# Delta scan with one key product per pair of heads, and separate semaphores for bonus and gate

## The reference

```python
def wkv7_scan(S0, r, w, k, v, a, b):
    def step(S, inp):
        r_t, w_t, k_t, v_t, a_t, b_t = inp
        sa = jnp.einsum('bhij,bhj->bhi', S, a_t)
        S = S * w_t[:, :, None, :] + sa[..., None] * b_t[:, :, None, :] + v_t[..., None] * k_t[:, :, None, :]
        return S, jnp.einsum('bhij,bhj->bhi', S, r_t)

# in rwkv_mixer, after the scan
    y = ((y - mean) * lax.rsqrt(var + RW_LN_EPS)).reshape(B, T, D) * ln_w + ln_b
    y = y + (jnp.sum(r * k * r_k.astype(f32), axis=-1, keepdims=True) * v).reshape(B, T, D)   # bonus
    out = (y.astype(h.dtype) * g) @ wo                                                        # gate
```

## Time and profile before

| | us |
|---|---|
| median of three runs | 3667.14 |
| profiled execution, its time | 3673.35 |
| profiled execution, its span | 3671.6 |
| PE busy | 3480.9 (95%) |
| delta scan, from the first memset to the last DMA issue | 2268.4 to 2449.6 of the span |
| the stage behind it, to the start of the next block | 2454.5 to 2515.8 of the span |

### The profile page before, as it was taken

The page is one execution under the profiler, slowest core; times in us unless marked ns, Lnnn a source line. Parts: engine busy times, 40 slices in busy tenths (PEclk is TensorE's granted clock), DMA queues, the critical chain, the costliest instruction groups (busy, mean ns, idle before and its releaser), DMA issues. The chain is left out here.

```text
span 3671.6 us, 60425 instructions
## 1 busy us (share of the span) xinstructions
PE 3480.9 (95%) x25874; PEld 3264.4 (89%) x25874; DVE 1516.0 (41%) x2519; ACT 1133.6 (31%) x2132; POOL 603.4 (16%) x724
## 2 busy tenths in 40 slices
PE   8899979999999999998899996987999999999998
PEld 8898769989999999995598795866998999999997
DVE  6335464343332332335326666555334332232233
ACT  6323263223220220224535532554223321121123
POOL 1100112002110110111312366423101110010012
PEclk9999989999999999998899997999999999999999
DMA  6411311201111111114646777963200111111111
GB/s 224 114 58 60 106 36 49 81 18 41 47 47 47 47 47 46 47 41 117 226 151 204 244 203 162 246 152 83 92 24 29 47 47 47 46 47 47 47 40 66
DMA packets 461158, 323.17 MB, mean 88 GB/s; under 512 B 108871, under 2 KB 438951, under 8 KB 457607
## 3 DMA queue, kind: packets, MB, share of 16 engines
q1 hardware_dynamic: 405645, 280.65, 26.5%
q10 hardware_dynamic: 44878, 19.14, 2.1%
q0 software_dynamic: 10368, 19.51, 1.6%
HBM read 232.32 MB, written 87.01 MB: 87 GB/s over the span
## 5 line engine op out<-in xcount | busy, mean ns | idle before, releaser
L83 PE MATMUL ps<-am_y,am_wh 128*128 128x352 f32 x4944 | 1182.9, 322 | 16.0 <-PEq L2631 16.0
L83 PE MATMUL ps<-am_h,am_wh 128*128 128x352 f32 x3648 | 887.7, 325 | 1.2 <-DVE am_h L1415 1.2
L83 PEld LDWEIGHTS ps<-am_y,am_wh 128*128 128x128 f32 x4944 | 856.4, 188 | 18.1 <-issue 16.8
L83 PE MATMUL ps<-am_y,am_wl 128*128 128x352 f32 x2472 | 792.8, 321 | 0.0
L83 PEld LDWEIGHTS ps<-am_h,am_wh 128*128 128x128 f32 x3648 | 639.8, 189 | 4.3 <-DVE am_h L1415 1.4
L83 PE MATMUL ps<-am_h,am_wl 128*128 128x352 f32 x1824 | 590.4, 324 | 0.0
L83 PEld LDWEIGHTS ps<-am_y,am_wl 128*128 128x128 f32 x2472 | 464.2, 188 | 0.0
L83 PEld LDWEIGHTS ps<-am_h,am_wl 128*128 128x128 f32 x1824 | 344.3, 189 | 0.0
L1503 POOL TENSOR_TENSOR am_silu<-am_silu,rs 128x352 f32<-128x352 f32 x132 | 126.8, 962 | 1229.2 <-ACT am_silu L1359 1229.2
L1085 DVE TENSOR_TENSOR x<-ps,x 128x352 f32<-128x352 f32 x240 | 125.9, 525 | 466.3 <-PE ps L83 460.7
L917 ACT ACTIVATE am_wh<-am_w 128x1024 fp32r<-128x1024 f32 (+1 forms) x184 | 189.5, 1030 | 378.2 <-PE ps L83 372.9
(11 more groups left out here) (340 smaller groups left out, 4581.3 us busy)
## 6 DMA issues: line engine op xcount, KB each, us to landing
am_w<-in_ffn_w SPq DMA_DIRECT2D x120, 512.0 KB, 3.8
rw_ra_d<-tb_rk SPq DMA_DIRECT2D x8, 1056.0 KB, 7.9
rw_kbt_d<-tb_gk SPq DMA_DIRECT2D x8, 1056.0 KB, 4.3
rw_gg_d<-tb_gk SPq DMA_DIRECT2D x8, 1056.0 KB, 6.5
fr_w<-in_xa_wk SPq DMA_DIRECT2D x8, 1024.0 KB, 5.8
fr_w<-in_xa_wv SPq DMA_DIRECT2D x8, 1024.0 KB, 5.4
am_w<-in_xa_wq SPq DMA_DIRECT2D x16, 512.0 KB, 3.8
am_w<-in_xa_wo SPq DMA_DIRECT2D x16, 512.0 KB, 3.8
```

Of the source, the lines that this page charges most:

```text
L83: mm = nc.tensor.matmul(out, l, part, start=start and n == 0, stop=stop and n == 2)
```

## The change

The keys `kbt` get an axis for the head: a pair's block is now 128 rows by 128 columns, with the two heads' keys on the diagonal and zeros elsewhere. The key product is one matmul for a pair. For that each slot of `kbt` is cleared once before its first use (first in `clear`), and the keys of a load come with one DMA for each head and chunk: four, two for load 0, in place of one. In `delta_post` bonus and gate get semaphores of their own: DVE waits for the bonus alone, POOL for the gate alone, and SP reloads a bonus buffer once pair p-2 is shifted, a gate buffer once it is gated.

```diff
-        g_in, ra_in, kbt, v = (sb(s, SLOTS, PAIRS, 2, HD) for s in ("g_in", "ra_in", "kbt", "v"))
+        g_in, ra_in, v = (sb(s, SLOTS, PAIRS, 2, HD) for s in ("g_in", "ra_in", "v"))
+        kbt = sb("kbt", SLOTS, PAIRS, 2, 2, HD)
...
+        rest_due = lambda l: 16 * (6 * loads(l) - (2 if l % SLOTS == 0 else 0))
...
         def clear(ops, at):
+            ops.memset(kbt[:, at], 0.0).then_inc(keys_cleared[at], 1)
             ops.memset(tt[:, at], 0.0).then_inc(tt_cleared[at], 1)
             ops.memset(v[:, at], 0.0).then_inc(v_cleared[at], 1)
...
-                sp.dma_start(kbt[:, l % SLOTS, :, 0:w, :], kbt_d[:, :, c:c + w, :].rearrange("p r c x -> r p c x"))\
-                    .then_inc(rest_in[l % SLOTS], 16)
+                if l < SLOTS:
+                    sp.wait_ge(keys_cleared[l], 1)
+                for h in range(2):
+                    r = slice(h * HD, (h + 1) * HD)
+                    for sub in range(w):
+                        sp.dma_start(kbt[r, l % SLOTS, :, sub, h, :], kbt_d[:, r, c + sub, :].rearrange("p r x -> r p x"))\
+                            .then_inc(rest_in[l % SLOTS], 16)
...
                     for p in range(4 * q, 4 * q + 4):
-                        for h in range(2):
-                            r, at = side[h], p % 4 * HD
-                            mm = nc.tensor.matmul(ps[r, 2 + 2 * q, at:at + HD], kbt[r, l % SLOTS, p, sub, :], vu[r, p, :],
-                                                  start=True, stop=True)
+                        at = p % 4 * HD
+                        mm = nc.tensor.matmul(ps[:, 2 + 2 * q, at:at + HD], kbt[:, l % SLOTS, p, sub].rearrange("r h j -> r (h j)"), vu[:, p, :],
+                                              start=True, stop=True)
                     mm.then_inc(s_done, 1)
...
             for p in range(n):
-                if p >= 2:
-                    sp.wait_ge(gated, 2 * (p - 1))
-                for j, src in enumerate((bonus_d, g_d)):
+                for j, (src, got, free) in enumerate(((bonus_d, bonus_in, shifted), (g_d, gate_in, gated))):
+                    if p >= 2:
+                        sp.wait_ge(free, 2 * (p - 1))
                     for s in range(2):
                         head = p // 2 * 4 + 2 * s + p % 2
                         sp.dma_start(inp[s * HD:(s + 1) * HD, p % 2, j], src[head * HD:(head + 1) * HD, 0:SEQ])\
-                            .then_inc(tile_in[p % 2], 16)
+                            .then_inc(got[p % 2], 16)
...
-                pool.wait_ge(tile_in[p % 2], 64 * (p // 2 + 1))
+                pool.wait_ge(gate_in[p % 2], 32 * (p // 2 + 1))
...
-                dve.wait_ge(tile_in[p % 2], 64 * (p // 2 + 1))
+                dve.wait_ge(bonus_in[p % 2], 32 * (p // 2 + 1))
```

More of the change, by code:

```diff
@@ L448, in delta_scan @@
         heads_in, init_in, init_turned, init_set = sem("heads_in"), sem("init_in"), sem("init_turned"), sem("init_set")
-        tt_cleared, v_cleared = ([sem(f"{t}_cleared{s}") for s in range(SLOTS)] for t in ("tt", "v"))
+        tt_cleared, v_cleared, keys_cleared = ([sem(f"{t}_cleared{s}") for s in range(SLOTS)] for t in ("tt", "v", "keys"))
         opened = sem("opened")
@@ L455, in delta_scan @@
         end_turned, end_out, stored, x_in, ln_in = (sem(s) for s in ("end_turned", "end_out", "stored", "x_in", "ln_in"))
-        ROWS, REST, OPENS = 2, 3, 4
+        ROWS, OPENS = 2, 4
         block = ctx.enter_context(nc.Block())
@@ L550, in _ @@
                 S = state[:, which(n)]
-                pe.wait_ge(rest_in[l % SLOTS], 16 * REST * loads(l))
+                pe.wait_ge(rest_in[l % SLOTS], rest_due(l))
                 pe.wait_ge(opened, OPENS * (n + 1))
@@ L606, in _ @@
                     nc.vector.tensor_copy(z[:, 2 * q:2 * q + 2, :], bank(q, 2)).then_inc(z_out, 1)
-                dve.wait_ge(rest_in[l % SLOTS], 16 * REST * loads(l))
+                dve.wait_ge(rest_in[l % SLOTS], rest_due(l))
                 for q in range(2):
@@ L2449, in delta_post @@
         centre = sb("centre", P)
-        tile_in, new_landed = [sem("in0"), sem("in1")], sem("new_landed")
+        bonus_in, gate_in = ([sem(f"{t}{s}") for s in range(2)] for t in ("bonus_in", "gate_in"))
+        new_landed = sem("new_landed")
         eps_set, centre_set, centred, squares, sums, logs, scales, scaled, shifted, gated, highs, lows = (
```

## The result

The median after is 3686.8 us (3684.16 to 3690.53, four runs) against 3666.84 before: a ratio of 1.0048, 95% interval [1.0036, 1.006]. I had predicted 3662.4, range 3655 to 3672. The change is slower, and outside my range. The profiled execution's span is 3688.8 us against 3671.6, 17.2 us more; it is the slowest of the four after.

A forecast was written before the change was run, and what follows sets the result against it. The scan was taken as bound by a PE-DVE loop of 4.50 us a step, the stage behind by DVE's DMA waits. Terms -0.7 + 3.0 - 7.0 = -4.7 us, from 3667.14 to 3662.4; range 3655 to 3672.

The forecast's parts named there:

- The key product on PE: Scan step: 16 wide passes replace 32, first half ready at 0.70 to 0.71 us; -0.7 us, bounds -3 to +1.7.
- My own sign of being wrong: Scan: the forecast is wrong if the step changes by more than 0.1 us from 4.50; 4.48 was expected.
- The 0.22 us stall: Scan step: PE's product with the state waits 0.22 us for the second half's decay, absorbing PE savings behind the first half.
- The start, +3.0: Scan up to step 7: slower key DMAs cost 2.2 us, load 0's wait 0.7; +3.0 us, bounds 0 and +7.
- 7.5 of 9.0 us: DMA queue from load 6 on: a load's share rises from 6.9 to about 7.5 of 9.0 us, costed at nothing.
- The rival of a queue that bounds the whole scan: Whole scan: from 2.1 us extra a load every load is late; +14 us, 3681, chance 12%.
- "issue" stalls, 0: PE's waits in the scan: fewer passes make them rarer, a fuller queue longer; 0, bounds 4.5 us either side.
- Bonus and gate, -7.0: Stage behind the scan: separate semaphores remove most of DVE's 9.4 us DMA wait; -7.0 us, range -3 to -9.
- the rival in which POOL leaves only -3: Stage behind the scan: POOL's loop of about 5 us a pair becomes the bound; sum -0.7 us, 3666.4, chance 21%.
- PE's idle time would fall to 9 us: Stage behind the scan: PE's idle time before the next block, expected at 9 us instead of 16.

The follow-up runs named there:

- e5: Kernel before, DMAs and layout kept, but the key product of steps 1 to 32 is one 128 by 128 matmul per pair (wrong values); ratio 1.0049.
- e3: e2 with its DMAs, memsets and layout, but the key product again as two 64 by 64 matmuls per pair on the diagonal blocks; 3674.2 us, ratio 1.0008.
- e9: Kernel before with the key product made for the first head of each pair only, 16 passes in one quarter of the array; 3673.96 us, one run.
- e10: Kernel before with head 0's key product issued twice instead of head 1's, all 32 passes in one quarter of the array; 3691.66 us, one run.
- e2: Kernel before with only the scan's part of the change, delta_post as before; 3688.83 us, ratio 1.0051.
- e6: Kernel before with its key load split into four DMAs of 256-byte runs, into the old compact layout, products as before; ratio 1.001.
- e1: Kernel before with only the separate semaphores for bonus and gate, scan untouched; 3662.0 us, ratio 0.9976.
- e7: e1 with the 4.2 MB load of x issued behind load 10 instead of load 3; ratio 0.9977.
- e4: Kernel before with the loop over heads outside the loop over a half's pairs in the key product, same 32 passes; 3672.28 us, ratio 1.001.

## Why the prediction was wrong, by its own steps

- **The key product on PE (failed).** "Half as many passes, each nearly twice as long: 0.04 us a step on PE" took L574's spacing for that of a full-array pass. 16 passes need 1.93 us to the next group, not 1.04, and the first half is ready at 1.14 us, not 0.71. Instead of -0.7 us the term is 33 x 0.745 = +24.6, of which the 26 steps from step 7 on, 19.4, reach the time: step 7 starts when its data comes, in e5 with the longer steps no later than before (51.4 us against 51.8). e3, e5, e9 and e10 show the cause: lost overlap of two quarters. The term is larger than all others and outside every bound I had given, since all bounds came from rows in which passes overlap; a rival with full-array passes (eight per half at 0.11) would have stood at about +24 and decided the sign. My own sign of being wrong, a step changed by more than 0.1 us, is the one that came.
- **What lies behind the stall.** The 0.22 us stall was read rightly, and it did go; but it is worth 0.22 us against 0.85, and DVE's copy of `z` is late next (0.18), a wait that I had not named.
- **The start, +3.0.** The mechanism was right, the size low: step 7 comes 5.2 us later in after, 4.1 in e2, 5.6 in e3, and in e6, with the DMAs alone, 4.3. (After's own 5.2 is not the DMAs' alone: there SP also stands 4.3 us for PE ahead of load 3's keys, against 1.8 at most in e2, while PE's first two steps take 9.4 and 9.3 us at the low clock.) The queue's share with steps of 4.50 is 94.7% (e3), above the 83% that 7.5 of 9.0 us says. The rival of a queue that bounds the whole scan did not come: with steps of 4.50 us the one wait behind step 7 is 0.2 us (e6).
- **"issue" stalls, 0 (failed too).** My bound, 4.5 us, was one row of four: PE's "issue" waits in before's scan are 9.5 us in all. In after they are 0.2. From step 7 on, before takes 8.3 us more than 26 x 4.50 (125.3 us), and after 9.9 more than 26 x 5.244 (146.3 us); of these 9.9, 8.8 lie in steps 7 to 9, which take 9.4, 9.3 and 5.9 us at the low clock. So the longer steps gave back nearly what the low clock took, and 19.4 of the 21.0 us measured are the steps'. That the two cancel was luck, and neither was in my sum. e3, at 4.50 us a step, has 4.9 us of "issue" waits, and e9, at 4.48 with 16 passes fewer, none. What they wait for stays open.
- **Bonus and gate, -7.0.** Right in mechanism, -5.8 in after and -6.1 in e1; the rival in which POOL leaves only -3 did not come. DVE's waits for DMA fell from 9.4 us to 1.2:

```profile
L2594 DVE SCALAR_TENSOR_TENSOR rw_y<-rw_y,rw_ln,do_in 128x512 f32<-128x512 f32 x13 | 14.4, 1106 | 1.6 <-DMA do_in<-rw_bonus_d 1.2
...
L2590 DVE SCALAR_TENSOR_TENSOR rw_y<-ps,rw_ln,do_rs 128x512 f32<-128x512 f32 x12 | 8.9, 742 | 1.2 <-ACT do_rs L2552 1.2
```

  A new wait of 1.2 us for ACT stands at L2590, and the mean length of the shift rose from 1007 to 1106 ns. The bonus now goes out when its buffer's last pair is shifted (DVE's L2594 at 2502.53 takes 0.75 us, SP issues at 2503.31), the gate at 2505.82. I had said PE's idle time would fall to 9 us from 16.0; it fell to 13.1, though the block ended 5.8 us sooner, because PE's own last work moved forward with it:

```profile
PE ps L83 <- PEq L2639: 13.1, 1, 13.1
```

What beats both kernels is the semaphores alone, e1: 0.9976 [0.9965, 0.9986] of before (e7, which adds the later `x`, is the same).

## What to carry to other kernels

Before joining small matmuls into one, look at whether they run side by side now: divide a group's busy time by its count and compare with the mean of one. Here a spacing of a third (L574) or a quarter (L584) of the mean meant two streams, and a single stream showed a ratio of 1.6 to 2.2 (L591, e9, e10). With two streams the "extra" instruction was free, and eight matmuls padded with zeros took 1.93 us where sixteen small ones had taken 1.08. And a price for a new shape must come from a row in which the pass fills the array in the same way, not from one with the same number of columns.

One semaphore over several transfers makes the first consumer wait for the slowest transfer and the reload for the last consumer; splitting both waits by consumer gave 6 us here.

## What the runs showed of the hardware

- Spacing in float32, with 64 moving columns and the clock at 2.4 GHz: 64 by 64 passes in one quarter come every 58 ns (e9, e10), full 128 by 128 ones every 111 ns (after, e5); two quarters (L584), or two halves (L574, L543), each keep their own pace beside each other (before).
- The order of independent matmuls in PE's list is worth time: the same 16 take 1.08 us alternating (before) and 1.46 in blocks of four (e4).
- 524 KB of keys in runs of 256 bytes and four DMAs instead of one raised the queue's share from 76.6% to 92.5% (e6): 1.4 us a load, not the 0.55 that the rates of the earlier trace rows gave. (e1, with the old DMAs, has 79.5% in the same window, so the 1.4 is good to 0.3.)
